# Both gate pieces side by side in products of 64 columns, also for the fourth quarter of the chunks

## The chip, the cores and the metric

The kernel runs on one core of one Trainium2 chip. The metric is the device time of one execution in microseconds (us), lower being better. Five engines of the core run their own instruction streams and meet at semaphores: TensorE (PE in the rows, its weight loads PEld) multiplies matrices, VectorE (DVE) and ScalarE (ACT) work elementwise, GpSimd (POOL) helps a little, SyncE (SP) starts the DMAs.

## The reference

The program is a chain of three transformer blocks on 256 tokens of width 1024 in float32. The change lies in the mixture of experts that the second block applies twice (two layers). Each layer has 16,384 experts, numbered by a pair of keys out of 128 x 128. For each token, 8 heads choose 16 experts each:

```python
def peer_ffn(h, wq, keys, u, v):            # shortened
    q = (h @ wq).reshape(B, S, PEER_HEADS, 2, half)
    s1, s2 = scores of both halves of q against the two sets of 128 keys
    v1, i1 = lax.top_k(s1, PEER_TOPK); v2, i2 = lax.top_k(s2, PEER_TOPK)
    sc, j = lax.top_k(every v1 + v2, PEER_TOPK)
    experts = e1 * PEER_NKEYS + e2          # the two key numbers that j picks
    gates = jax.nn.softmax(sc, axis=-1)
    act = gelu(einsum('td,ted->te', h, u[experts]))
    return einsum('te,ted->td', gates * act, v[experts])
```

## The kernel before, in words

The kernel does not gather experts. It computes `gelu(h @ u)` for all 16,384 of them in 128 chunks of 128 experts (the experts lie on the partitions, the 256 tokens in the free dimension), multiplies each value by the gate of its expert and token, which is zero for nearly all, and multiplies the result with `v`. The class `Experts` is that stage; there are two in the program.

**Halves.** The stage has 256 steps, called halves: 128 "in" halves that make hidden chunks from `u`, and 128 "out" halves that add a hidden chunk times `v` to the sums in `acc`. `expert_order` puts in 0 to 63 first, then out c and in c + 64 in turn, then out 64 to 127. Every float32 weight is split in a high and a low part (`w_hi` by ScalarE, L1116; `w_lo` by VectorE, L1124), and each product is made of three. The split weights lie in a ring of three buffers: ScalarE's highs of half g wait until TensorE has begun what follows half g - 3 (`halves_used`). The hidden chunk of an out half is split too: its high by ScalarE (L2157), its low by VectorE (L2190), one half ahead.

**Gates.** The gates must become a dense array of experts x tokens. The chunks are taken in four quarters of 32 chunks, and the tokens in 16 batches of 16. For a batch VectorE builds one-hots in fp16 (`build`, L2244 to L2255): `hot2`, 128 columns per token, says which second key each of the token's 128 chosen pairs has, and `hot1`, 32 columns per token, holds the gate at the pair's first key. The gate is split in two fp16 pieces, so there are two arrays `hot1`. TensorE multiplies them token by token (`spread`, L2121): the result, for a token 128 experts x 32 chunks, is the sum over both pieces. Three halves later VectorE multiplies it into the hidden values (`multiply`, L2258).

**Two forms.** In quarters 0 and 3 (counting from 0) a token takes two products of 32 columns that add up in PSUM, 32 products for a batch in one bank, batches alternating between banks 2 and 3. VectorE multiplies straight from PSUM. In the quarters of `BESIDE`, 1 and 2, a token takes one product of 64 columns, both pieces side by side, 16 products for a batch, 8 tokens in each of banks 2 and 3. ScalarE copies the second pieces to SBUF (`take_seconds`, L2206), VectorE adds the first pieces from PSUM to them into `whole` (L2266, once per bank), and the product with the hidden values reads `whole` (L2276).

**When.** `__init__` (L2012) lays the 16 batches of a quarter evenly between the last in half that the quarter needs and the first out half that uses it. Quarter 3 has halves 195 to 219 for that, 24 halves, all of them out halves; quarters 1 and 2 have 56. A batch is built by VectorE in its step g, spread by TensorE after half g, and multiplied in VectorE's step g + 3. The spread waits for the one-hots and for its bank: the semaphore `gated` counts what VectorE has read out of the banks (`lay_out_banks`, L2038, works out the counts). In each step VectorE does in turn: lows of the half (L1124), hidden low of the next (L2190), the sum of a returned in chunk (L2195, only up to half 193), multiply, build.

Of the kernel before, what the change touches and what calls it, by code (L numbers as in the profile page):

```python
# [73 lines left out]
class Chip:  # L74


    def __init__(self, ctx, nc):
# [64 lines left out]
        self.onehots_made = ctx.enter_context(nc.semaphore("onehots_made"))  # L142
        self.gate_banks = ctx.enter_context(nc.semaphore("gate_banks_filled"))
        self.seconds_out = ctx.enter_context(nc.semaphore("second_pieces_out"))
        self.quarters_gated = ctx.enter_context(nc.semaphore("quarters_gated"))
        self.gated = ctx.enter_context(nc.semaphore("hidden_gated"))
        self.heads_normed = ctx.enter_context(nc.semaphore("heads_normed"))
        self.heads_gated_early = ctx.enter_context(nc.semaphore("heads_gated_by_pool"))
# [94 lines left out]
class Stage:  # L243
# [19 lines left out]
    def scalar(self, act):  # L263
        pass
# [815 lines left out]
class SplitWeights(Stage):  # L1080
# [6 lines left out]
    QUARTER = HALF_SLOT // 2  # L1087
# [884 lines left out]
QUARTER = CHUNKS // 4  # L1972
BATCH = BANK // QUARTER
BATCHES = S // BATCH
# [12 lines left out]
class Experts(SplitWeights):  # L1987
# [2 lines left out]
    WIDEN_AT = 15  # L1990
    EXP_AT = 23
    TURN_AFTER = 33
    BESIDE = (1, 2)

    def __init__(self, k, route, found, hidden, gate, rest, places, pairs, pieces, hot1, hot2, mask, whole,
                 second):
# [41 lines left out]
    def lay_out_banks(self):  # L2038
# [3 lines left out]
        for q in range(4):  # L2042
            for b in range(BATCHES):
                n = 2 if q in self.BESIDE else 1
                for half in range(n):
# [75 lines left out]
    def spread(self, pe, q, b):  # L2121
        k = self.k
        pe.wait_ge(k.onehots_made, self.batches_through(q, b))
        for first, n, bank, free, units, through in self.fills[q, b]:
            if free:
                pe.wait_ge(k.gated, free)
            for j in range(first, first + n):
                hot2, hot1 = self.hot2[b % 2][:, j, :], self.hot1[b % 2]
                if q in self.BESIDE:
                    w = PIECES * QUARTER  # L2130
# [14 lines left out]
    def scalar(self, act):  # L2145
        k = self.k
        for g in range(self.n + 2):
            if self.ahead <= g < self.n:
                self.split_high(act, g)
            if g + 1 < self.n and self.halves[g + 1][0] == "out":  # L2150
                c = self.halves[g + 1][1]
                if c % QUARTER == 0:
                    if c // QUARTER in self.BESIDE:
                        act.wait_ge(k.quarters_gated, self.number * len(self.BESIDE) + 1 + self.BESIDE.index(c // QUARTER))
                    else:
                        act.wait_ge(k.gated, self.units_through[c // QUARTER, BATCHES - 1])
                act.activation(self.top(c), self.place(c), ACT.Copy).then_inc(k.tops_made, 1)  # L2157
            for q, batch in self.spread_after[g - 3]:
                if q in self.BESIDE:
                    self.take_seconds(act, q, batch)  # L2160
            if self.WIDEN_AT <= g < self.WIDEN_AT + 8:
                self.route.widen(act, g - self.WIDEN_AT)
            if g == self.EXP_AT:
                self.route.scalar(act)
            if 2 <= g and self.halves[g - 2][0] == "in":
                c = self.halves[g - 2][1]
                act.wait_ge(k.hidden_banks, self.chunks_before() + c + 1)
                if c < PLACES:
                    act.activation(self.place(c), k.bank[:, c % 2, 0:S], ACT.Gelu).then_inc(k.hidden_made, 1)  # L2169
                else:  # L2170
                    act.activation(self.place(c), k.bank[:, c % 2, S:2 * S], ACT.Copy).then_inc(k.hidden_rests, 1)  # L2171
            if 3 <= g and self.halves[g - 3][0] == "in" and self.halves[g - 3][1] >= PLACES:
                c = self.halves[g - 3][1]
                act.wait_ge(k.hidden_added, self.added_through(c))
                act.activation(self.place(c), self.place(c), ACT.Gelu).then_inc(k.hidden_made, 1)

    def vector(self, dve):
# [3 lines left out]
        for g in range(self.n):  # L2181
# [18 lines left out]
                self.build(dve, q, batch)  # L2200
            self.sum_step(dve, g)

    def seconds_through(self, q, b):
        return 2 * (BATCHES * (self.number * len(self.BESIDE) + self.BESIDE.index(q)) + b + 1)

    def take_seconds(self, act, q, b):  # L2206
        k = self.k
# [50 lines left out]
    def multiply(self, dve, q, b):  # L2258
        k = self.k
        first = q * QUARTER % PLACES  # L2260
        for t, n, bank, free, units, through in self.fills[q, b]:
            dve.wait_ge(k.gate_banks, through)
            if q in self.BESIDE:
                pieces = k.bank[:, bank, :].rearrange("p (t i n) -> p i t n", t=n, i=PIECES)
                dve.wait_ge(k.seconds_out, self.seconds_through(q, b) + (t > 0) - 1)
                dve.tensor_tensor(self.whole[:, t:t + n, :], pieces[:, 0], self.second[:, t:t + n, :],  # L2266
                                  ALU.add).then_inc(k.gated, units)
        if b == 0:
            dve.wait_ge(k.hidden_made, self.chunks_before() + (q + 1) * QUARTER)
        hidden = self.hidden[:, first:first + QUARTER, b * BATCH:(b + 1) * BATCH]  # L2270
        if q in self.BESIDE:
            dve.wait_ge(k.gated, self.units_through[q, b])
            gates = self.whole.rearrange("p t n -> p n t")
        else:
            gates = k.bank[:, 2 + b % 2, :].rearrange("p (t i) -> p i t", t=BATCH)
        ins = dve.scalar_tensor_tensor(hidden, gates, 1.0 / GATE_SCALE, hidden, ALU.mult, ALU.mult)  # L2276
        if q not in self.BESIDE:
            ins.then_inc(k.gated, 2)
        elif b == BATCHES - 1:
            ins.then_inc(k.quarters_gated, 1)  # L2280

# [1551 lines left out]
```

## Time and profile before

| what | value |
|---|---|
| median of 3 timed runs | 3816.76 us (3811.96 to 3827.05) |
| the profiled execution's own time | 3812.13 us |
| its span, first to last instruction | 3810.3 us |
| mean granted TensorE clock | 0.968 |
| ScalarE, busy share of the span | 54% |
| out halves and gates of quarter 3, first stage | 2104 to 2192 us |
| the same in the second stage | 3094 to 3182 us |

A share of busy time is an average over many stages with different limits. For a change in one place one reads the windows and the order of time there. Times in rows are microseconds from the start of the span; an instruction's duration holds its start-up and drain, so that the distance between the starts of two neighbours is what one of them costs its engine.

### The profile page before, as it was taken

Reading aid. Unit: us, or ns where it says so; the run is one execution under the profiler, and the core shown is the slowest. Engines: PE = TensorE matmul, PEld = TensorE weight load, DVE = VectorE, ACT = ScalarE, POOL = GpSimd, SP = SyncE. Lnnn points to the kernel's source line nnn. Section 1 sums busy time; section 2 is a strip of 40 time slices with the busy share of each in tenths; the row PEclk is TensorE's granted clock in tenths of the full one; section 3 lists DMA queues with packets and bytes.
Section 4 is the critical chain, followed back from the end, with each engine's and each line's share of the span. In section 5 each row is a group of like instructions: output and inputs, shape, how many; then the busy total and the mean of one; then the engine's idle time right before and its main releaser. Section 6 shows DMA issues by size and latency. Waiting matters only on the chain. (4 is left out here: it accounts for less than half of the span.)

```text
span 3810.3 us, 59916 instructions
## 1 busy us (share of the span) xinstructions
PE 3637.0 (95%) x22328; PEld 3116.2 (82%) x22328; DVE 3061.5 (80%) x6382; ACT 2060.6 (54%) x4449; POOL 122.1 (3%) x112
## 2 busy tenths in 40 slices
PE   6999999999889979999999999999999999999898
PEld 5887788887778767998888887799988888888687
DVE  7887688887678776988888956689798997788766
ACT  3554555555355545545656456554555655555455
POOL 0000000000000000400000000050000000000000
PEclk9999999999789989999999999999999999999899
DMA  8767375766247523544454454254455545686354
GB/s 325 277 243 287 125 295 209 299 221 240 100 181 268 213 85 138 184 156 177 178 185 180 166 188 156 78 177 159 174 177 179 181 172 178 232 308 261 122 188 155
DMA packets 119619, 744.52 MB, mean 195 GB/s; under 512 B 13857, under 2 KB 14273, under 8 KB 44833
## 3 DMA queue, kind: packets, MB, share of 16 engines
q1 hardware_dynamic: 118082, 737.57, 52.9%
q8 instruction: 178, 2.92, 0.3%
q10 hardware_dynamic: 416, 2.06, 0.1%
q0 software_dynamic: 832, 1.06, 0.1%
q14 instruction: 111, 0.91, 0.1%
HBM read 738.53 MB, written 1.05 MB: 194 GB/s over the span
## 5 line engine op out<-in xcount | busy, mean ns | idle before, releaser
L212 PE MATMUL bank<-h_split,weights_high 128*128 128x512 f32 (+1 forms) x5824 | 1714.7, 358 | 15.5 <-DVE h_split L723 9.4
L1116 ACT ACTIVATE weights_high<-weight_ring 128x512 fp32r<-128x512 f32 x2248 | 1292.6, 624 | 650.9 <-PE bank L212 377.1
L1124 DVE TENSOR_TENSOR weights_low<-weight_ring,weights_high 128x512 fp32r<-128x512 f32 x2168 | 1394.9, 687 | 274.5 <-ACT weights_high L1116 252.9
L212 PE MATMUL bank<-h_split,weights_low 128*128 128x256 f32 x4800 | 1269.2, 280 | 0.0
L212 PEld LDWEIGHTS bank<-h_split,weights_high 128*128 128x128 f32 x5824 | 1014.8, 189 | 163.4 <-issue 16.7
L212 PEld LDWEIGHTS bank<-h_split,weights_low 128*128 128x128 f32 x4800 | 911.1, 190 | 37.8
L212 PE MATMUL acc<-weights_high,hidden_high 128*128 128x512 f32 x1552 | 613.8, 395 | 2.6 <-DVE hidden_low L1298 2.4
L212 PE MATMUL acc<-weights_high,hidden_low 128*128 128x512 f32 x1552 | 605.0, 390 | 0.0
L212 PE MATMUL acc<-weights_low,hidden_high 128*128 128x512 f32 x1552 | 604.5, 390 | 0.0
L212 PEld LDWEIGHTS acc<-weights_high,hidden_low 128*128 128x128 f32 x1552 | 291.3, 188 | 63.9
L212 PEld LDWEIGHTS acc<-weights_low,hidden_high 128*128 128x128 f32 x1552 | 291.7, 188 | 59.8 <-issue 0.2
L212 PEld LDWEIGHTS acc<-weights_high,hidden_high 128*128 128x128 f32 x1552 | 291.3, 188 | 56.2 <-issue 4.2
L1263 ACT ACTIVATE work<-bank 128x256 f32<-128x256 f32 x264 | 101.8, 386 | 344.9 <-PE bank L212 344.9
L212 PE MATMUL bank<-weights_high,h_split 128*128 128x512 f32 x704 | 222.8, 395 | 7.4 <-DVEq L234 2.9
L212 PEld LDWEIGHTS bank<-weights_high,h_split 128*128 128x128 f32 x704 | 133.6, 190 | 38.8 <-DVEq L234 3.9
L2249 DVE TENSOR_TENSOR h_tok<-h_feat,work 128x2048 f16<-128x2048 f16 x128 | 156.0, 1219 | 0.0
L2169 ACT ACTIVATE work<-bank 128x256 f32<-128x256 f32 x128 | 49.2, 384 | 193.2 <-PE bank L212 193.2
L212 PE MATMUL bank<-work 128*128 128x64 f32 (+10 forms) x896 | 125.6, 333 | 19.5 <-ACTq L234 8.3
L212 PE MATMUL bank<-weights_low,h_split 128*128 128x512 f32 x352 | 138.3, 393 | 0.0
L212 PEld LDWEIGHTS bank<-work 128*128 128x128 f32 (+5 forms) x896 | 108.0, 213 | 35.4 <-ACTq L234 11.1
L2171 ACT ACTIVATE work<-bank 128x256 f32<-128x256 f32 x128 | 49.3, 385 | 141.2 <-PE bank L212 141.2
L348 DVE SCALAR_TENSOR_TENSOR mod_sums<-h_tok,columns,mod_sums 128x512 f32<-128x512 f32 x160 | 112.5, 746 | 15.5 <-DMA h_tok<-slots 14.8
(347 smaller groups left out, 3522.1 us busy)
## 6 DMA issues: line engine op xcount, KB each, us to landing
weight_ring<-stream SPq DMA_DIRECT2D x574, 1024.0 KB, 4.8
h_feat<-slots SPq DMA_DIRECT2D x96, 512.0 KB, 5.8
h_tok<-slots SPq DMA_DIRECT2D x94, 512.0 KB, 5.9
work<-slots SPq DMA_DIRECT2D x26, 512.0 KB, 8.4
mod_sums<-biases SPq DMA_DIRECT2D x7, 1536.0 KB
h_feat<-rows SPq DMA_DIRECT2D x8, 512.0 KB, 3.8
work<-rows SPq DMA_DIRECT2D x7, 512.0 KB, 4.7
work<-biases SPq DMA_DIRECT2D x1, 1536.0 KB
```

Source lines behind the costliest of these rows:

```text
L212: ins = self.nc.tensor.matmul(out, lhs, rhs, start=start, stop=stop)
L348: ins = dve.scalar_tensor_tensor(self.sums.where[:, a], k.buffers[self.buffer][:, h * BANK:(h + 1) * BANK], c, self.sums.where[:, a], ALU. ...
L1116: act.activation(k.w_hi[:, b, q * self.QUARTER:(q + 1) * self.QUARTER], self.raw(g, q), ACT.Copy).then_inc(k.highs_ready, 1)
L1124: return eng.tensor_tensor(k.w_lo[:, b, w], self.raw(g, q), k.w_hi[:, b, w].bitcast(F32), ALU.subtract)
L1263: act.activation(self.rests[:, part, :], self.bank_of(c, part)[:, S:2 * S], ACT.Copy).then_inc(k.scalar_for_vector.sem, k.scalar_for_vecto ...
L2169: act.activation(self.place(c), k.bank[:, c % 2, 0:S], ACT.Gelu).then_inc(k.hidden_made, 1)
L2171: act.activation(self.place(c), k.bank[:, c % 2, S:2 * S], ACT.Copy).then_inc(k.hidden_rests, 1)
L2249: dve.tensor_tensor(cut(hot2), grid(self.places, N_KEYS), spread(self.pairs[:, S + b * BATCH:S + (b + 1) * BATCH, :], N_KEYS), ALU.is_equal)
```

## The change

`BESIDE` becomes (1, 2, 3): quarter 3 takes the form of quarters 1 and 2. Per stage, for 16 batches, that is 256 products of 64 columns in place of 512 of 32, 32 copies by ScalarE that were not there, 32 sums by VectorE that were not there, and 16 products by VectorE that read `whole` in SBUF where they read PSUM. Every batch of the quarter fills both banks.

The semaphore `quarters_gated` (one signal per quarter) is replaced by `sums_gated` (one per batch). Before the first sum of a batch VectorE now waits until its product of the batch before has read `whole`, and ScalarE waits on the same semaphore before the first out chunk of a quarter.

```diff
-        self.quarters_gated = ctx.enter_context(nc.semaphore("quarters_gated"))
+        self.sums_gated = ctx.enter_context(nc.semaphore("summed_gates_used"))
...
-    BESIDE = (1, 2)
+    BESIDE = (1, 2, 3)
...
-                        act.wait_ge(k.quarters_gated, self.number * len(self.BESIDE) + 1 + self.BESIDE.index(c // QUARTER))
+                        act.wait_ge(k.sums_gated, self.sums_through(c // QUARTER, BATCHES - 1))
...
+    def sums_through(self, q, b):
+        return BATCHES * (self.number * len(self.BESIDE) + self.BESIDE.index(q)) + b + 1
...
+                if t == 0 and self.sums_through(q, b) > 1:
+                    dve.wait_ge(k.sums_gated, self.sums_through(q, b) - 1)
...
-        elif b == BATCHES - 1:
-            ins.then_inc(k.quarters_gated, 1)
+        else:
+            ins.then_inc(k.sums_gated, 1)
```

VectorE in the fourth quarter, one step with a multiply and a build. First before; `work<-bank,work` is the product with the hidden values, `h_tok` is `hot2`:

```order
L1124 TENSOR_TENSOR weights_low<-weight_ring,weights_high 128x512 [waits highs_ready] x2
L2190 TENSOR_TENSOR hidden_low<-work,hidden_high 128x256 [waits weighted_highs_made]
L2276 SCALAR_TENSOR_TENSOR work<-bank,work 128x32x16 [waits gate_banks_filled]
L2244 TENSOR_TENSOR work<-h_feat,work 128x512
L2249 TENSOR_TENSOR h_tok<-h_feat,work 128x2048 [waits gate_banks_filled]
L2255 TENSOR_TENSOR work<-work 128x16x32 [waits dve_step]
L2255 TENSOR_TENSOR work<-work 128x16x32
```

The same step in the changed kernel, where line numbers are up to 5 higher:

```order
L1124 TENSOR_TENSOR weights_low<-weight_ring,weights_high 128x512 [waits highs_ready] x2
L2190 TENSOR_TENSOR hidden_low<-work,hidden_high 128x256 [waits weighted_highs_made]
L2271 TENSOR_TENSOR work<-bank,work 128x256 [waits second_pieces_out,summed_gates_used,gate_banks_filled]
L2271 TENSOR_TENSOR work<-bank,work 128x256 [waits second_pieces_out,gate_banks_filled]
L2281 SCALAR_TENSOR_TENSOR work<-work 128x32x16 [waits hidden_gated]
L2247 TENSOR_TENSOR work<-h_feat,work 128x512
L2252 TENSOR_TENSOR h_tok<-h_feat,work 128x2048 [waits gate_banks_filled]
L2258 TENSOR_TENSOR work<-work 128x16x32 [waits dve_step]
L2258 TENSOR_TENSOR work<-work 128x16x32
```

Two sums have come ahead of the product, which reads SBUF alone, and three waits with them. The steps around stand as they stood.

TensorE in the fourth quarter between two out halves, before; `work,h_tok` are the one-hots:

```order
L212 MATMUL acc<-weights_high,hidden_low 128x512
L212 MATMUL bank<-work,h_tok 128x32 [waits hidden_gated,onehots_made]
L212 MATMUL bank<-work,h_tok 128x32 x31
L212 MATMUL acc<-weights_high,hidden_high 128x512 [waits weighted_lows_made,first_lows_by_vector]
L212 MATMUL acc<-weights_low,hidden_high 128x512
```

And in the changed kernel:

```order
L212 MATMUL acc<-weights_high,hidden_low 128x512
L212 MATMUL bank<-work,h_tok 128x64 [waits hidden_gated,onehots_made]
L212 MATMUL bank<-work,h_tok 128x64 x7
L212 MATMUL bank<-work,h_tok 128x64 [waits hidden_gated]
L212 MATMUL bank<-work,h_tok 128x64 x7
L212 MATMUL acc<-weights_high,hidden_high 128x512 [waits weighted_lows_made,first_lows_by_vector]
```

The 32 products are 16, in two groups of which each waits for its bank. The name of the wait is the same, but its count is another: it was that of the batch two before, and is that of the batch just before.

## Rows read from the trace of the kernel before

**Rows 1.** The page: busy time, share of the span, instructions.

```profile
PE 3637.0 (95%) x22328; PEld 3116.2 (82%) x22328; DVE 3061.5 (80%) x6382; ACT 2060.6 (54%) x4449; POOL 122.1 (3%) x112
```

**Rows 2.** Windows: stretch, us, busy (count) of each engine, clock, DMA share, GB/s.

```profile
2113.30:2180.10 66.80, 66.80 (x659) 54.72 (x658) 66.52 (x126) 29.21 (x60) 0.00 (x0) 1.00 0.44 159
2104.39:2189.93 85.54, 85.54 (x826) 70.05 (x824) 83.69 (x158) 38.58 (x80) 0.00 (x0) 1.00 0.46 165
3093.92:3179.47 85.55, 85.55 (x826) 70.05 (x825) 83.69 (x158) 38.59 (x80) 0.00 (x0) 1.00 0.44 165
```

**Rows 3.** Order of time on TensorE, fourth quarter: start, duration, what, count.

```profile
2129.65 0.39 PE L212 MATMUL acc<-weights_high,hidden_low 128*128 128x512 f32 x1
2129.88 0.96 PE L212 MATMUL bank<-work,h_tok 128*128 128x32 f16 x32
2130.69 0.47 PE L212 MATMUL acc<-weights_high,hidden_high 128*128 128x512 f32 x1
2131.01 0.39 PE L212 MATMUL acc<-weights_low,hidden_high 128*128 128x512 f32 x1
```

**Rows 4.** Order of time on VectorE, fourth quarter, idle time before in brackets.

```profile
2111.75 1.29 DVE L1124 TENSOR_TENSOR weights_low<-weight_ring,weights_high 128x512 fp32r<-128x512 f32 x2
...
2113.29 0.69 DVE L2276 SCALAR_TENSOR_TENSOR work<-bank,work 128x512 f32<-128x512 f32 x1
2113.89 0.41 DVE L2244 TENSOR_TENSOR work<-h_feat,work 128x512 f16<-128x512 f16 x1
...
2116.03 1.29 DVE L1124 TENSOR_TENSOR weights_low<-weight_ring,weights_high 128x512 fp32r<-128x512 f32 x2
...
2181.09 1.29 DVE L1124 TENSOR_TENSOR weights_low<-weight_ring,weights_high 128x512 fp32r<-128x512 f32 x2 [0.28 <-ACT weights_high L1116]
2186.32 0.69 DVE L2276 SCALAR_TENSOR_TENSOR work<-bank,work 128x512 f32<-128x512 f32 x1
...
2189.98 1.29 DVE L1124 TENSOR_TENSOR weights_low<-weight_ring,weights_high 128x512 fp32r<-128x512 f32 x2 [0.89 <-ACT weights_high L1116]
```

**Rows 5.** Order of time on VectorE in the third quarter.

```profile
2023.67 0.42 DVE L2195 TENSOR_TENSOR work<-bank,work 128x256 f32<-128x256 f32 x1 [1.35 <-ACT work L2171]
2024.01 0.74 DVE L2266 TENSOR_TENSOR work<-bank,work 128x256 f32<-128x256 f32 x2
2024.79 1.11 DVE L2276 SCALAR_TENSOR_TENSOR work<-work 128x512 f32<-128x512 f32 x1
2025.81 1.29 DVE L1124 TENSOR_TENSOR weights_low<-weight_ring,weights_high 128x512 fp32r<-128x512 f32 x2
```

**Rows 6.** Order of time on TensorE in the second quarter.

```profile
1735.46 0.64 PE L212 MATMUL bank<-work,h_tok 128*128 128x64 f16 x16
1735.94 0.48 PE L212 MATMUL acc<-weights_high,hidden_high 128*128 128x512 f32 x1
```

**Rows 7.** Line 2212: minimum, median, maximum in ns, first and last start.

```profile
L2212 ACT ACTIVATE work<-bank x128: 360/375/387, 1737.0 to 3078.6; 128x256 f32<-128x256 f32 x128
```

**Rows 8.** Order of time on ScalarE, fourth quarter.

```profile
2130.17 1.15 ACT L1116 ACTIVATE weights_high<-weight_ring 128x512 fp32r<-128x512 f32 x2 [1.06 <-PE bank L212]
```

**Rows 9.** TensorE behind the spread of batch 1: half 2 begins.

```profile
2114.31 0.47 PE L212 MATMUL acc<-weights_high,hidden_high 128*128 128x512 f32 x1
```

**Rows 10.** TensorE behind the last spread: half 25 begins.

```profile
2189.85 0.47 PE L212 MATMUL acc<-weights_high,hidden_high 128*128 128x512 f32 x1
```

**Rows 11.** VectorE behind the quarter; one row of a repeated pattern.

```profile
2199.27 1.29 DVE L1124 TENSOR_TENSOR weights_low<-weight_ring,weights_high 128x512 fp32r<-128x512 f32 x2 [1.09 <-ACT weights_high L1116]
```

**Rows 12.** Windows with and behind an idle piece of TensorE.

```profile
2294.40:2296.80 2.40, 0.57 (x3) 0.52 (x4) 2.00 (x4) 2.37 (x6) 0.00 (x0) 0.99 0.00 0
2296.80:2300.20 3.40, 3.40 (x10) 2.63 (x9) 2.89 (x5) 0.64 (x2) 0.00 (x0) 0.50 0.54 164
```

**Rows 13.** Line 2276: minimum, median, maximum in ns, first and last start.

```profile
L2276 DVE SCALAR_TENSOR_TENSOR work<-bank,work x64: 676/684/689, 1639.5 to 3181.1; 128x512 f32<-128x512 f32 x64
L2276 DVE SCALAR_TENSOR_TENSOR work<-work x64: 1103/1114/1140, 1738.7 to 3079.9; 128x512 f32<-128x512 f32 x64
```

More of the change, by code:

```diff
@@ L2201, in vector @@
             self.sum_step(dve, g)
+    def sums_through(self, q, b):
+        return BATCHES * (self.number * len(self.BESIDE) + self.BESIDE.index(q)) + b + 1
     def seconds_through(self, q, b):
-        return 2 * (BATCHES * (self.number * len(self.BESIDE) + self.BESIDE.index(q)) + b + 1)
+        return 2 * self.sums_through(q, b)
     def take_seconds(self, act, q, b):
```

## The prediction

> **What bounds the kernel now.** I read the page's busy times first, then the windows, then the order of time on each engine.
>
> The page has TensorE busy for 95% of the span and VectorE for 80% [rows 1]. That says which engine is short on average, and not which one is short where the change acts. The change acts on the fourth quarter of the chunks in both expert stages. The windows there show both engines full: in 66.80 us TensorE is busy for all of it and VectorE for 66.52, while ScalarE has 29.21 [rows 2]. The second expert stage reads the same: the window of 85.54 us and its twin of 85.55 us hold the same 826 matmuls and 158 VectorE instructions, with 83.69 us of VectorE each [rows 2]. So I work out one stage and double it.
>
> In order of time TensorE runs without a gap through that stretch: 12 products of a half, and after 16 of 24 halves the 32 small products of a batch [rows 3]. VectorE also has almost no gap, and its rows repeat per half: two weight lows and a hidden low, then, where a batch falls due, the multiply (L2276) and the building of one-hots (L2244 to L2255) [rows 4]. TensorE sets the pace, by a hair. The reader is to see that VectorE has no room at this place: its idle pieces in the stretch are like the one of 0.28 us, and reach 0.89 only at the end [rows 4].
>
> **Why this quarter is tight.** I count halves of the stretch from 0, the one after which the first of the 16 batches is spread (half 195 of the stage). The code spaces batches by 24/15 halves, so they are spread after halves 0, 1, 3, 4, 6, 8, 9, 11, 12, 14, 16, 17, 19, 20, 22, 24, and multiplied in VectorE's step three halves on (3, 4, 6, ... 27). In quarters two and three, which already have the new form, the spacing is 56/15 halves, and VectorE has idle pieces of 1.35 us there [rows 5].
>
> **The costs, each from a distance between starts.**
>
> - VectorE, lows and hidden low of a half: 2111.75 to 2113.29 is 1.54 us. Build of a batch: 2113.89 to 2116.03 is 2.14. Multiply of the old form: 2113.29 to 2113.89 is 0.60 [rows 4].
> - Multiply of the new form, in the third quarter: 2024.01 (two sums) to 2025.81 (the next work) is 1.80: 0.78 for two sums and the wait on them, 1.02 for the product that reads both operands from SBUF [rows 5]. VectorE therefore gains 1.20 us of work per batch, 19.2 per stage.
> - TensorE, half: 2114.31 to 2189.85 holds 23 halves and 14 batches [rows 9, 10], (75.54 - 14 x 0.90) / 23 = 2.74. The 0.90 is the small products of a batch, old form: 2129.88 to 2130.69 is 0.81, and the next product is 0.09 late (2130.69 to 2131.01 is 0.32, where 0.23 is usual), so 0.90 [rows 3]. New form: 2×8 products, 1735.46 to 1735.94 is 0.48, with the same 0.09, so 0.57 [rows 6]. It saves 0.33 per batch.
> - ScalarE: two copies more per batch, 0.375 us each [rows 7], on an engine with 37 us idle in 66.8 [rows 2]. They stand behind the weight highs and the hidden high of the same step. In the fourth quarter ScalarE has 1.06 or more idle after those [rows 8]. I cost them at nothing; if that cover went, one copy (0.375) per batch would be late, 6 us per stage.
> - The wait on the last product before a new sum: the product is at least one half's lows (1.54) old by then. In the third quarter the two satisfied waits before the first sum leave it 0.34 behind its predecessor (2023.67 to 2024.01) [rows 5], as without a wait. Nothing, there and here.
> - The ring of small-product banks: a batch of the new form fills both banks, so it waits for the sums of the batch just before; a batch of the old form alternates and waits for the one two before. Behind the waiting TensorE instruction stand all later halves, and ScalarE's next weight highs wait for those. This wait is what carries VectorE's load to TensorE. Batch 1 is spread after half 1, but the sums of batch 0 come in VectorE's step 3.
>
> **The sum.** Start where both kernels agree. In the old form half 2 begins at 2114.31, behind the small products of batch 1 [rows 9]. In the new form these wait for the second sum of batch 0, which ends 0.74 after 2113.29, and eight products take 0.24: half 2 begins at 2114.3. No loss yet, and no gain from the shorter products.
>
> From there the last spread that waits is batch 15 (after half 24), on the sums of batch 14 in VectorE's step 25. Between the multiplies of batches 0 and 14 VectorE does 14 multiplies x 1.80 = 25.2, 14 builds x 2.14 = 30.0 and 22 halves' lows x 1.54 = 33.9: 89.0 us. TensorE today needs 2114.31 to 2189.85 = 75.5 for the same halves [rows 9, 10]. So half 25 begins 13.5 us later. The same count with 0.60 in place of 1.80 gives 72.2, against 73.03 between the starts 2113.29 and 2186.32 [rows 4]; the method is 0.8 us off by the idle pieces.
>
> Then TensorE has its pace back: halves 25 and 26 take 2.74 each, and VectorE's two remaining steps with one multiply (1.54 + 1.54 + 1.80) fit beside them. Nothing returns the time later, since halves 29 and on are paced by TensorE, with VectorE idle 1.09 in each [rows 11]. VectorE could also be made to wait for weight highs, which need TensorE to begin what follows the half three before. At batch 3 (after half 4) its products wait for the sums of batch 2 in VectorE's step 6, at 2113.29 + 1.80 + 2.14 + 1.54 (step 4) + 1.80 + 2.14 + 1.54 (step 5) + 1.54 = 2125.8, done at 2126.2. ScalarE starts 0.29 after such products do (2129.88 to 2130.17) and has two pieces in 1.15 [rows 3, 8], the first at 2127.1; VectorE wants it at its step 7, 1.80 + 2.14 later than 2125.8, at 2129.7. The margin is 2.6 us, and at batch 6, the other long wait, it is the same. Two stages: 27 us.
>
> **What TensorE's waits cost besides.** TensorE would idle 89.0 - 23 x 2.74 - 14 x 0.57 = 18.0 us per stage, mostly in five gaps of about 3 to 3.6 us (before batches 3, 6, 8, 11, 13, which are the ones due two steps behind). The trace shows what such a gap does: TensorE has 0.57 us of work in 2.40 us, and then a granted clock of 0.50 for 3.40 us [rows 12]. That is the 1.2 GHz level, and loses 1.7 us of TensorE's work; for a longer gap I allow twice that, 3.4. From below it costs nothing, since the next wait is as long as the loss; from above, all ten gaps at 3.4 us add up to 34. I take 2 us for both stages, near the lower end, since a loss shortens the gap behind it. The page "TensorE: Matmul & The Clock Gate" of the Trainium skill (Part 1) has the same behaviour as its rule, an idle array being throttled to half rate; it speaks against this change, and the trace agrees with its direction.
>
> The sum: 3812.13 (profiled execution, 1.8 over its span) + 27 + 2 = 3841. The three timed runs of before have a median of 3816.76, 4.6 above it; I predict 3842.
>
> **One price where the Trainium skill differs.** The trace has the product from PSUM at a median of 684 ns and the same product from SBUF alone at 1114 ns, 64 of each [rows 13]. "VectorE: DVE Perf Modes" (the section on the TRN2 errata) gives fp32 from PSUM the larger fixed cost, 120 cycles against 58. By it the move to SBUF would be free; the row decides. The sum without that extra is the third rival.
>
> **The rivals.**
>
> 1. Faster. TensorE sets the pace and its products shrink by 0.33 us in each of 32 batches: 3812.1 - 10.6 = 3801.5. For it: TensorE has no idle time in the stretch, and VectorE stands at 80% overall. Against it: 66.52 of 66.80. It decides if VectorE's 1.20 us per batch fit beside; they need 19.2 us, and 85.5 - 83.7 = 1.9 are free [rows 2].
> 2. Much slower: the gaps before the products lower TensorE's clock, and the losses add up instead of vanishing in the next wait: 3841 + 32 = 3873 at the most, 3857 if half do.
> 3. Less slow: the product from SBUF costs 0.60 here, since it reads differently than in the third quarter. Then the multiply is 1.38, the sum 89.0 - 14 x 0.42 = 83.2, the loss 7.6 per stage: 3827. Against it: all 64 rows lie within 1103 and 1140.
> 4. The change does not reach the path: the waits for banks are met because TensorE lags. Then nothing changes, 3812 to 3817. Against it: VectorE's step 25 would have to be early, with 16.8 us more work ahead of it.
>
> **How the numbers follow.** Forecast 0.79; rival 1 0.04, rival 2 0.08, rival 3 0.05, rival 4 0.04. A measurement tells this kernel from no change by about 0.5%, 19 us: below 3798 and above 3836. The forecast's own range is 3834 to 3852 (24 to 34 us for the two stages' sum, and the 4.6 between execution and median); some 0.05 of it falls under 3836. Slower: 0.74 + 0.08 + a little of rival 3 = 0.83. Faster: 0.04. Same: 0.13. The range for 8 in 10 takes in rival 3 and half of rival 2: 3825 to 3858.
>
> **What would show it.** In the profile after: the fourth quarter is 13 to 15 us longer in each stage (about 99 where 85.5 stood), with VectorE busy over 98% and TensorE near 80%; TensorE waits before small products on the sums, five times over 2 us per stage; the product from SBUF is there 32 times more at 1.11 us; the clock reads 0.50 for some microseconds inside; all other stages are unchanged. Wrong if VectorE shows idle pieces on weight highs in that quarter (then the ring of waits is tighter than its load), if TensorE shows no waits there, or if the clock stays low past the quarter.

## The result and the profile after

| | before | changed |
|---|---|---|
| median of 7 timed runs | 3812.28 us (3807.51 to 3827.83) | 3844.57 us (3838.93 to 3859.42) |
| ratio, 95% interval | | 1.0083 (1.0056 to 1.0109) |
| the profiled execution | 3812.13 us | 3844.57 us |
| S of the first and second expert stage | 75.53, 75.53 us | 89.93, 89.08 us |

The change makes the kernel 0.83% slower, some 32 us. S is the measure of all that follows: the time on TensorE from the start of half 2 to the start of half 25 of the fourth quarter, as the prediction counts them. It is read to 0.01 us in one profile, while whole executions of one kernel scatter by 20 us. The like stretch of the first quarter, which is the same in every kernel of this document, measures 72.80 us in each of them.

The page of the changed kernel, against [rows 1]. TensorE has 512 matmuls fewer, VectorE 64 instructions more and 36 us more to do, and the shares hardly moved:

```profile
PE 3638.8 (95%) x21816; PEld 3113.4 (81%) x21816; DVE 3097.8 (81%) x6446; ACT 2082.2 (54%) x4513; POOL 122.0 (3%) x112
```

The windows over S in both stages of the changed kernel (columns as in [rows 2]):

```profile
2122.34:2212.27 89.93, 74.66 (x507) 59.51 (x503) 89.45 (x166) 41.24 (x98) 0.00 (x0) 0.96 0.39 134
3124.68:3213.77 89.09, 76.36 (x507) 60.64 (x503) 88.61 (x165) 41.26 (x98) 0.00 (x0) 0.94 0.38 137
```

VectorE is busy for all but 0.48 us of each. TensorE, which had no idle time there in [rows 2], works for 74.7 of 89.9 and 76.4 of 89.1 us. Who waits for whom in the first of the two windows (total us, times, the longest; VectorE has no row, so it waits for nobody):

```profile
ACT weights_high L1116 <- PE bank L212: 34.6, 15, 5.0
PEld bank L212 <- issue: 19.9, 14, 3.9
ACT weights_high L1116 <- PE acc L212: 16.1, 9, 2.8
PE bank L212 <- DVE work L2271: 15.3, 7, 3.5
```

The last row is where the loss shows: TensorE waits 15.3 us for VectorE's sums. Add 3.4 us that it loses at half clock (below) and take off the 14 x 0.33 = 4.6 that its products have become shorter, and 14.1 of the 14.4 us by which this S is longer are accounted for. In order of time, the small products of batch 3 of the first stage, where the old form has no gap (compare [rows 3]):

```profile
2130.97 0.39 PE L212 MATMUL acc<-weights_high,hidden_low 128*128 128x512 f32 x1
2134.42 0.65 PE L212 MATMUL bank<-work,h_tok 128*128 128x64 f16 x16 [3.06 <-DVE work L2271]
2134.90 0.47 PE L212 MATMUL acc<-weights_high,hidden_high 128*128 128x512 f32 x1
```

VectorE in the same stretch, against [rows 4]: no row has an idle piece. The multiply in these rows is 2126.86 to 2128.64, that is 1.78 where 0.60 stood; a build 2.13; lows and hidden low 1.54. The last row is the pair of sums that batch 3 waits for; it begins as soon as VectorE gets to it, and the products begin at 2134.42, behind the first sum:

```profile
2125.32 1.28 DVE L1124 TENSOR_TENSOR weights_low<-weight_ring,weights_high 128x512 fp32r<-128x512 f32 x2
2126.52 0.41 DVE L2190 TENSOR_TENSOR hidden_low<-work,hidden_high 128x256 fp32r<-128x256 f32 x1
2126.86 0.74 DVE L2271 TENSOR_TENSOR work<-bank,work 128x256 f32<-128x256 f32 x2
2127.63 1.09 DVE L2281 SCALAR_TENSOR_TENSOR work<-work 128x512 f32<-128x512 f32 x1
2128.64 0.41 DVE L2247 TENSOR_TENSOR work<-h_feat,work 128x512 f16<-128x512 f16 x1
2128.97 1.22 DVE L2252 TENSOR_TENSOR h_tok<-h_feat,work 128x2048 f16<-128x2048 f16 x1
2130.10 0.75 DVE L2258 TENSOR_TENSOR work<-work 128x512 f16<-128x512 f16 x2
2130.77 1.29 DVE L1124 TENSOR_TENSOR weights_low<-weight_ring,weights_high 128x512 fp32r<-128x512 f32 x2
...
2132.31 1.29 DVE L1124 TENSOR_TENSOR weights_low<-weight_ring,weights_high 128x512 fp32r<-128x512 f32 x2
2133.52 0.42 DVE L2190 TENSOR_TENSOR hidden_low<-work,hidden_high 128x256 fp32r<-128x256 f32 x1
2133.85 0.75 DVE L2271 TENSOR_TENSOR work<-bank,work 128x256 f32<-128x256 f32 x2
```

ScalarE's copies lie where the prediction put them, behind the highs, with idle time before the next ones (compare [rows 8]):

```profile
2140.74 1.16 ACT L1116 ACTIVATE weights_high<-weight_ring 128x512 fp32r<-128x512 f32 x2 [1.07 <-PE bank L212]
2141.80 0.40 ACT L2157 ACTIVATE hidden_high<-work 128x256 fp32r<-128x256 f32 x1
2142.11 0.64 ACT L2215 ACTIVATE work<-bank 128x256 f32<-128x256 f32 x2
2144.25 1.16 ACT L1116 ACTIVATE weights_high<-weight_ring 128x512 fp32r<-128x512 f32 x2 [1.50 <-PE acc L212]
```

And the clock. Windows of the changed kernel around two waits of TensorE (3.55 us before batch 6, 2.98 before batch 13):

```profile
2150.40:2153.40 3.00, 0.00 (x0) 0.00 (x0) 3.00 (x7) 0.00 (x0) 0.00 (x0) 1.00 0.01 3
2153.40:2156.80 3.40, 2.89 (x21) 2.54 (x22) 3.37 (x7) 2.00 (x5) 0.00 (x0) 0.50 0.33 43
2195.40:2197.80 2.40, 0.03 (x1) 0.00 (x0) 2.40 (x6) 0.00 (x0) 0.00 (x0) 1.00 0.66 277
2197.80:2201.20 3.40, 2.79 (x21) 2.43 (x22) 3.37 (x7) 2.00 (x5) 0.00 (x0) 0.50 0.02 5
```

TensorE idles through the first and third window, and in the second and fourth it runs at 0.50, the 1.2 GHz level. That makes 6.8 us at half rate in S of the first stage and 10.2 us in the second.

**Where the 32 us are.** The same instruction on TensorE, before and after, gives the shift from the front of the span. It is 8.0 us at the first small products of the fourth quarter of the first stage (2109.85 and 2117.85), and 7.9 already at 1491 us, ahead of any expert stage, where no instruction differs: these two executions differ there by that much on their own. From there to half 25 it grows by 14.4 us (2189.85 and 2212.27). In the second stage it goes from 20.8 (3099.39 and 3120.19) to 34.4 (3179.38 and 3213.77), by 13.6. Nothing of it comes back behind the quarter: the shift is 22.42 at half 25 of the first stage and still 22.44 a hundred microseconds later. The two quarters account for 28.0 of the 32.5 us between the spans; the rest arises in stretches where no instruction differs, and is scatter.

### The profile page after: what moved, and what is told of

Same layout as the page of the kernel before. It is cut to its first block and busy times, and to the rows that moved or that the text cites. A ratio compares the mean times of both kernels' runs of the same rounds, so it can differ in the third digit from the quotient of the medians.

```text
span 3842.8 us, 59118 instructions
## 1 busy us (share of the span) xinstructions
PE 3638.8 (95%) x21816; PEld 3113.4 (81%) x21816; DVE 3097.8 (81%) x6446; ACT 2082.2 (54%) x4513; POOL 122.0 (3%) x112
## 5 line engine op out<-in xcount | busy, mean ns | idle before, releaser
L2171 ACT ACTIVATE work<-bank 128x256 f32<-128x256 f32 x128 | 49.4, 386 | 140.8 <-PE bank L212 140.8
```

## The experiments

Each has one execution with a profile. The whole times hold the scatter named above, so the verdicts are on S.

### The new semaphore alone

```diff
-    BESIDE = (1, 2, 3)
+    BESIDE = (1, 2)
```

(on the changed kernel)

> The new semaphore alone: the fourth quarter keeps the old form, and the second and third quarters have the new wait of VectorE on the product of the batch before. All theories measure S, the time on TensorE from the start of half 2 to the start of half 25 of the fourth quarter: 75.5 us before, 89.9 and 89.1 us in the changed kernel. Theory (VectorE's added load of 1.2 us per batch sets the pace): S is 75.5 in both stages, and the third quarter is as before. Rival (the wait itself costs, in every quarter that has it): S is 75.5 too, but the stretch of the second and third quarter is over 1 us longer per stage and VectorE shows idle time on its own semaphore.

S is 75.53 in both stages, the same to the last digit as before:

```profile
2117.33:2192.86 75.53, 75.53 (x731) 61.86 (x727) 73.76 (x138) 33.59 (x70) 0.00 (x0) 1.00 0.46 161
3106.87:3182.40 75.53, 75.53 (x730) 61.85 (x727) 73.77 (x138) 33.59 (x70) 0.00 (x0) 1.00 0.45 162
```

The like stretch of the second and third quarter (the half behind batch 1 to the half behind batch 15) is 155.62 and 155.58 us, with 155.60 and 155.59 before. VectorE's list of waits between 1740 and 2110 us has ScalarE's copies of the in chunks (L2171) and its weight highs in it, and not its own semaphore. The wait costs nothing.

### The tighter ring of banks alone

```diff
                     freed[bank] = units
+                    if q == 3 and n == 1:
+                        freed[5 - bank] = units
```

(on the kernel before)

> The kernel before, but in the fourth quarter every batch of small products also waits for the multiply of the batch just before, as it would if it filled both banks: the tighter ring without the load. Theory (load): the multiplies of batches due two steps behind come 0.2 to 0.7 us after TensorE is ready for the next small products, so S grows from 75.5 by 2 to 4 us. Rival (the ring by itself costs the time, VectorE's load is a bystander): S is near 89.

S is 76.33 and 76.38: 0.8 us more, less than either side expected, and the profile shows a single wait of TensorE of 0.5 us. The ring alone is not the cost. The changed kernel's list of waits would have misled here: all of TensorE's waits stand there in the row of the ring's semaphore.

### Product of the fourth quarter cut to an eighth

```diff
+        if q == 3:
+            hidden, gates = hidden[:, :, 0:2], gates[:, :, 0:2]
         ins = dve.scalar_tensor_tensor(hidden, gates, 1.0 / GATE_SCALE, hidden, ALU.mult, ALU.mult)
```

> The changed kernel, but in the fourth quarter VectorE's product covers 2 of a batch's 16 tokens (so the hidden values of the others are not gated in that quarter): the full ring, the sums and ScalarE's copies stay, the product falls from 1.02 us to about 0.15. Theory (load): the multiply is 0.93, S = 14 x 0.93 + 30.0 + 33.9 = 76.9, within 1 us. Rival (ring): near 89, since all waits stay. Rival (ScalarE's copies are late): S stays over 82.

S is 78.22 in both stages: 11 us of the loss are gone with one operation of VectorE, all waits being as in the changed kernel. The 1.3 above the 76.9 worked out are these, VectorE's waits between 2110 and 2200:

```profile
DVE weights_low L1124 <- ACT weights_high L1116: 1.3, 2, 1.0
```

At this load the two engines are nearly level (TensorE would need 71.0), and then each waits for the other now and then.

### The sums done twice

```diff
+                if q == 3:
+                    spare = (self.rest if t else self.gate).rearrange("p (t n) -> p t n", n=QUARTER)
+                    dve.tensor_tensor(spare, pieces[:, 0], self.second[:, t:t + n, :], ALU.add)
                 dve.tensor_tensor(self.whole[:, t:t + n, :], pieces[:, 0], self.second[:, t:t + n, :],
```

> The changed kernel with each of VectorE's sums of the fourth quarter done a second time into a spare tile: 0.68 us more of VectorE's work per batch, nothing else. Theory (load): S grows by 14 x 0.68 = 9.5 over the changed kernel, to about 98.8. Rival (TensorE's clock or the ring sets the pace, VectorE has room left): S grows by less than 3. The granted clock tells a third: if its drops add up, it falls below 1.00 for longer and S passes 101.

```profile
2114.30:2212.79 98.49, 80.67 (x507) 63.17 (x503) 98.01 (x193) 41.21 (x98) 0.00 (x0) 0.91 0.36 129
3127.66:3226.94 99.28, 82.56 (x506) 64.91 (x503) 98.80 (x194) 40.84 (x98) 0.00 (x0) 0.88 0.35 121
```

98.5 and 99.3 against 98.8. Every microsecond given to VectorE is paid in full (9.4 and 10.2 more for the 9.5 added). The clock falls further, to a mean of 0.91 and 0.88 over the stretch (17 and 24 us at half rate), and still the time is the one of VectorE's load within 0.5 us: TensorE's slack takes the slower halves up.

### The load alone, in the old form

```diff
+        if q == 3:
+            flat = k.bank[:, 2 + b % 2, :].rearrange("p (t n) -> p t n", n=QUARTER)
+            if b:
+                dve.wait_ge(k.dve_step, self.spared)
+            for t in (0, BATCH // 2):
+                at = slice(t, t + BATCH // 2)
+                dve.tensor_tensor(self.whole[:, at, :], flat[:, at], self.second[:, at, :], ALU.add)
+            spare = self.rest.rearrange("p (t n) -> p t n", n=QUARTER)
+            dve.tensor_tensor(spare, flat[:, 0:BATCH // 2], self.second[:, 0:BATCH // 2, :], ALU.add).then_inc(k.dve_step, 1)
+            self.spared = k.step("dve")
         ins = dve.scalar_tensor_tensor(hidden, gates, 1.0 / GATE_SCALE, hidden, ALU.mult, ALU.mult)
```

(on the kernel before: 32-column products, alternating banks, no copies by ScalarE)

> The kernel before (old form and old ring in the fourth quarter), with three more sums of 128x256 by VectorE per batch of that quarter, ahead of the multiply and into tiles that nobody reads there: 3 x 0.34 = 1.02 us more per batch, so a multiply of 1.62. Theory (the load alone does it, with or without the new ring, the 64-column products and ScalarE's copies): VectorE has 14 x 1.62 + 30.0 + 33.9 = 86.6 us to do and S is 86.6, within 1.5. Rival (the load needs the tighter ring to reach TensorE, or ScalarE's copies): S stays under 80.

```profile
2129.97:2214.90 84.93, 81.17 (x731) 64.35 (x727) 84.93 (x176) 33.60 (x70) 0.00 (x0) 0.96 0.41 144
```

S is 84.93 in both stages, VectorE busy without a break. It is 1.7 below the 86.6 expected, just past the margin, and the end of the stretch says why:

```profile
2209.87 1.30 DVE L1124 TENSOR_TENSOR weights_low<-weight_ring,weights_high 128x512 fp32r<-128x512 f32 x2
```
```profile
2211.22 0.50 PE L212 MATMUL acc<-weights_high,hidden_high 128*128 128x512 f32 x1
2214.08 0.96 PE L212 MATMUL bank<-work,h_tok 128*128 128x32 f16 x32
```

With alternating banks batch 15 (2214.08) does not wait, neither for a bank nor for its one-hots. TensorE is held up for the last time at half 24 (2211.22), by VectorE's lows of that half, and runs on for 3.7 us to half 25. VectorE's work in the path is then 14 multiplies of 1.60, 13 builds, 20 halves' lows and the two lows of half 24, 82.3 us from the first multiply, which begins 1.0 before half 2: 82.3 - 1.0 + 3.7 = 85.0. The load makes 9.4 us of loss by itself; form, ring and copies are not needed for it. What carries it to TensorE is another thing here: the listed waits are 2.1 us for one-hots and 1.4 for weight lows, and none for a bank.

### Turned tile of summed gates

```diff
-    whole, second = room(BATCH, QUARTER), room(BATCH, QUARTER)
+    whole, second = room(QUARTER, BATCH).rearrange("p n t -> p t n"), room(BATCH, QUARTER)
```

> The changed kernel with the tile of summed gates laid out chunk by token, so that VectorE's product reads it in one run per row instead of 512 values 128 bytes apart; the sums write it spread out instead. S is 89.0 to 89.9 in the changed kernel. If the 1.02 us of the product from SBUF comes from the spread-out reads, it falls to near the 0.60 of the product from PSUM and S to 89.0 - 14 x 0.42 = 83.2. If it comes from two operands in SBUF alone, as in the other products of this kernel, it stays and S stays 89. If the spread-out writes cost the sums as much, S stays 89 too and the sums' rows show it.

Line 2281 and line 2271 of this run (minimum, median, maximum in ns):

```profile
L2281 DVE SCALAR_TENSOR_TENSOR work<-work x96: 691/693/695, 1755.6 to 3222.6; 128x512 f32<-128x512 f32 x96
L2281 DVE SCALAR_TENSOR_TENSOR work<-bank,work x32: 684/685/693, 1656.1 to 2730.7; 128x512 f32<-128x512 f32 x32
```
```profile
L2271 DVE TENSOR_TENSOR work<-bank,work x192: 579/605/637, 1754.5 to 3222.0; 128x256 f32<-128x256 f32 x192
```

Both answers at once. The product falls from 1115 to 693 ns, about what it costs from PSUM (685). But PSUM is read with the same stride: in both forms the gates of a chunk lie 32 values, 128 bytes, apart. So the extra is neither the memory nor the stride by itself, but this stride in SBUF. And the sums rise from 416 to 605 ns with their spread-out writes. By distances between starts, averaged over the 15 multiplies of the window, a sum goes from 0.39 to 0.54 and the product from 1.02 to 0.61, so the multiply from 1.81 to 1.69: 14 x 0.12 = 1.7. S is 87.44 and 87.48, 1.6 less than the changed kernel's 89.1. "SBUF — State Buffer" of the Trainium skill ("Door 1: The DMA port swizzle") has it as a rule that consecutive accesses within a 16-byte line of SBUF run at full rate and each step to a new line pays. The trace agrees for VectorE's reads (1115 against 693 ns) and for its writes (605 against 416).

### One sum in place of two

```diff
+        if q == 3:
+            dve.wait_ge(k.gate_banks, self.units_through[q, b])
+            dve.wait_ge(k.sums_gated, self.sums_through(q, b) - 1)
+            dve.wait_ge(k.seconds_out, self.seconds_through(q, b))
+            both = k.bank[:, 2:4, :].rearrange("p a n -> p (a n)").rearrange("p (t i n) -> p i t n", i=PIECES, n=QUARTER)
+            dve.tensor_tensor(self.whole, both[:, 0], self.second, ALU.add).then_inc(k.gated, 2)
...
```

> The changed kernel with one sum of 128x512 over both banks in place of two of 128x256 in the fourth quarter. If a VectorE instruction costs its elements at 0.26 us per 256 and the rest is a fixed part, the two sums with their 0.78 become about 0.60 and S = 89.0 - 14 x 0.18 = 86.5. Rival (the earlier release of the first bank by the first of two sums is worth more): S is 89 or over, since TensorE's first 8 products wait for the whole sum.

```profile
2141.66 0.69 DVE L2269 TENSOR_TENSOR work<-bank,work 128x512 f32<-128x512 f32 x1
2142.38 1.05 DVE L2287 SCALAR_TENSOR_TENSOR work<-work 128x512 f32<-128x512 f32 x1
```

S is 88.14 in both stages: a gain of 1.0, not 2.6. The sum with the wait on it takes 0.72 (2141.66 to 2142.38) where two took 0.78; I had put the whole of the 0.18 down to a second start. A sum that nothing waits on costs 0.33 in the run above with the load alone. In the changed kernel the first sum of a pair costs 0.33 too and the second, which the product waits on, 0.45; so 0.12 of the 0.78 is that wait, and it stays.

### Weight lows given to GpSimd

Two edits, the second with both pieces of a low (`BY_POOL = (0, 1)`), and one with the turned tile besides:

```diff
+    LATE, BY_POOL = range(196, 223), (1,)
...
+        for g in self.LATE:
+            for q in self.BY_POOL:
+                ins = self.low_piece(pool, g, q)
+            ins.then_inc(k.lows_by_pool, 1)
...
+            if g in self.LATE:
+                pe.wait_ge(k.lows_by_pool, self.pool_base + self.POOL_HALVES + g - self.LATE[0] + 1)
```

(and VectorE makes the pieces that are left)

> The changed kernel with GpSimd making the second of the two weight lows of a half in halves 196 to 222 (a piece takes 1.30 us there, 0.60 on VectorE), so 0.60 us less of VectorE's work per half. Theory (load): S = 89.0 - 22 x 0.60 = 75.8, near the kernel before. Rival (ring): S stays near 89. A third: the two engines slow each other while both work on SBUF, then VectorE's fp16 builds are over 2.14 us and S lies between.

> The same with GpSimd making both weight lows of those halves: VectorE's work falls by 1.20 per half to 25.2 + 30.0 + 22 x 0.34 = 62.7 us, less than the 71.0 that TensorE needs for 23 halves of 2.74 and 14 batches of 0.57. Theory: TensorE sets the pace, S is 71 to 73, less than the 75.5 of the kernel before. Rivals: GpSimd, at 2.6 us per half plus its start behind ScalarE's highs, becomes the bound (then S is over 76 and TensorE waits for its lows), or slows VectorE (builds over 2.14 us).

> The turned tile of summed gates and GpSimd's second weight low together. By the loads: 89.0 - 22 x 0.60 - 14 x 0.42 = 69.9 for VectorE if both edits do all they can, so TensorE's 71.0 is the bound and S is 71 to 73; if the turned tile brings nothing, S is as with GpSimd's help alone, near 75.8. Rival (ring): near 89.

S is 99.1, 108.9 (110.6 in the second stage) and 96.1: all slower than the changed kernel, where by the load all three were to win the time back. The whole executions, 3874, 3884 and 3868 us, are above those of the changed kernel as well. The windows over S with one and with both pieces on GpSimd:

```profile
2133.53:2232.64 99.11, 80.64 (x505) 63.77 (x502) 98.63 (x143) 41.10 (x98) 45.45 (x23) 0.90 0.36 128
```
```profile
2118.37:2227.27 108.90, 82.44 (x505) 65.00 (x502) 108.41 (x121) 40.83 (x98) 68.38 (x46) 0.90 0.32 110
```

VectorE has 23 and 45 instructions fewer and is busy for longer. Its order of time and GpSimd's, with one piece:

```profile
2140.23 1.47 DVE L2263 TENSOR_TENSOR work<-h_feat,work 128x512 f16<-128x512 f16 x1
2141.63 1.22 DVE L2268 TENSOR_TENSOR h_tok<-h_feat,work 128x2048 f16<-128x2048 f16 x1
2142.77 1.85 DVE L2274 TENSOR_TENSOR work<-work 128x512 f16<-128x512 f16 x2
...
2154.16 1.73 DVE L1124 TENSOR_TENSOR weights_low<-weight_ring,weights_high 128x512 fp32r<-128x512 f32 x1
```
```profile
2139.61 1.82 POOL L1124 TENSOR_TENSOR weights_low<-weight_ring,weights_high 128x512 fp32r<-128x512 f32 x1 [3.80 <-ACT weights_high L1116]
2142.16 1.83 POOL L1124 TENSOR_TENSOR weights_low<-weight_ring,weights_high 128x512 fp32r<-128x512 f32 x1 [0.74 <-ACT weights_high L1116]
```

GpSimd's first piece runs to 2141.43. VectorE's instruction of 0.41 us that begins at 2140.23 ends at 2141.70, just behind it. The next, of 1.22, begins in GpSimd's pause and takes 1.22, though the second piece begins under it at 2142.16; that piece takes 1.83 where 1.30 is usual, so it ends 1.30 behind 2142.69, about where VectorE's ends. Those of VectorE from 2142.77 then meet the second piece. So in these rows the one that starts first runs at its own time and the other ends late. The low of 0.68 us at 2154.16 takes 1.73. VectorE stands about 1.1 us in each of these, and GpSimd's pieces take 1.29 to 4.98 us, 1.98 on the average over the window. The third possibility of the first expectation came true, and stronger than it said. VectorE's time is 99.1 where its load is 75.8, so each of 23 pieces costs it 1.0 us; with both pieces it is 108.9 where the load is 62.7, again 1.0 for each of 46. A piece takes 0.60 off VectorE: the help costs more than the work it takes. TensorE waits on VectorE's sums and not on GpSimd in all three (18.4 us in the first). The "GPSIMD Engine Reference" of the Trainium skill (1. Specifications) says that GpSimd shares its SBUF interfaces with VectorE and meets its instructions with two SBUF inputs; the trace agrees, and it puts the price at 1.0 us of a piece that takes 1.30 alone.

### The changed kernel once more

> The changed kernel once more. In its first profile S was 89.93 in the first expert stage and 89.08 in the second, where VectorE's load is 89.04. If the 0.9 is the granted clock (two drops to 0.50 in each of the windows, at other places), S is again 89.0 to 90.5 and any excess over 89.1 stands where a drop fell into halves that no wait follows. If the first stage has a load of its own that the second has not, the same stage is again 0.9 longer.

S is 89.14 and 89.09, with 10.2 us at half rate in each. The 0.9 of the first profile's first stage was the clock: its second drop (the fourth window above) slows the halves behind batch 13, and in that execution the two batches left (14 and 15) came without a wait behind slower halves. From the products of batch 13 to those of batch 15 it is 13.38 us (2198.41 to 2211.79), and 12.48 in the second stage (3200.80 to 3213.28), where they run at full clock: these are the 0.9. The row of batch 15:

```profile
2211.56 0.39 PE L212 MATMUL acc<-weights_high,hidden_low 128*128 128x512 f32 x1
2211.79 0.64 PE L212 MATMUL bank<-work,h_tok 128*128 128x64 f16 x16
```

In the repeat the drops come after the gaps before batches 3, 6 and 11, and each is followed by a wait that takes it up.

## Why the prediction was right

- **Which engine is short.** Predicted: VectorE, over 98% busy in the quarter, TensorE near 80%. Measured: 99.5%, and 83 to 86%. Three experiments move S as VectorE's load says: the sums done twice add 9.4 and 10.2 us where 9.5 were worked out, the small product gives 78.22 where the load is 76.9 and VectorE waits 1.3, and the load alone in the old form gives 84.93 where 85.0 come out.
- **The sum.** Predicted: 89.0 us for the stretch, 13.5 more. Measured: 89.93 and 89.08, repeated 89.14 and 89.09. The multiply was taken from the third quarter at 1.80 and is 1.81 on the average over the window.
- **Where both kernels agree.** Half 2 begins 4.46 us behind the start of batch 0's products before (2109.85 to 2114.31) and 4.49 after (2117.85 to 2122.34): no loss yet and none of the saved 0.33, as said.
- **The waits.** Predicted: 18.0 us per stage, five of them over 2 us. Measured: 15.3 us in 7 waits in the first stage, four of them over 2 us, and 12.7 us in 7 waits in the second, three over 2 us. In place of the rest stand the slower halves: 6.8 and 10.2 us at half clock are 3.4 and 5.1 us of work. The gap before batch 8 shows it: 1.64 and 1.39 us where about 3 were forecast, behind a drop at batch 6.
- **The clock.** 2 us were added for it over both stages, near the lower end of 0 to 34. Measured: 0.9 in one stage of four seen, nothing in the others, while the clock was at half rate for 6.8 to 10.2 us in each. The reason given, that a loss shortens the gap behind it, is what the waits show.
- **The price of the product from SBUF.** The size was right, and what makes it was not known. The prediction read the row (1114 against 684) as SBUF against PSUM, set it against the comparison of the two in "VectorE: DVE Perf Modes" of the Trainium skill (the section on the TRN2 errata), and let the row decide. The turned tile shows that the 1114 belongs to reads 128 bytes apart in SBUF: in one run the product costs 693 from SBUF, and PSUM with the same stride costs 685. The number held here because the fourth quarter has the layout of the rows it came from.
- **The whole.** 3842 was predicted and 3844.57 measured. The two quarters were predicted at 27 us and 2 for the clock, and measured at 28.0; the rest of the agreement is luck within a scatter of 20 us.

## What to carry to other kernels

Look for the engine that is short in the stretch that changes, not in the span: an edit that saves 0.33 us per batch on the engine that is busy 95% overall cost 1.2 us on the one that was busy 99.6% just there. Work per turn times turns, between two points where both kernels agree, then gave the loss to within 1 us, and the same count says beforehand that a form for which VectorE has the time in a roomy quarter (56 halves for 16 batches) does not fit in a tight one (24). Whether it pays in the roomy ones no run here shows. In a list of waits the row names the semaphore that was late and not the reason: relax or tighten the wait and change the load apart from each other before naming either. None of the versions tried has a shorter S than the kernel before; of these, the fourth quarter is best left in the old form.

## What the runs showed of the hardware

- VectorE and GpSimd, both at work on SBUF: VectorE's instructions with two SBUF inputs, of 2 or of 4 bytes, that came second ended only behind GpSimd's (0.41 to 1.47, 0.68 to 1.73 us), and GpSimd's piece of 1.30, where it came second, ended late in turn (1.83 in the rows above). VectorE's sums with one operand in PSUM took 0.41 to 0.44 in the ten cases that overlap a piece in the first two of these runs.
- A VectorE product of 128x512 takes 693 ns with its second operand in one run in SBUF, 1115 with it 128 bytes apart in SBUF, and 684 with it 128 bytes apart in PSUM; a sum of 128x256 takes 416 with a contiguous and 605 with a spread-out target in SBUF.
- A VectorE instruction that waits on the one just before it begins 0.12 us later than one that does not (0.45 against 0.33 behind a sum of 128x256).
- TensorE's granted clock fell to 0.50 for 3.4 us behind waits of 2.4 to 3.6 us, but not behind each: in the first profile it stayed at 1.00 behind waits of 3.06 and 3.52 us (batches 3 and 11 of the first stage), and fell behind one of 2.54 (batch 6 of the second). Half rate for up to 24 of 99 us cost at most 0.5 us where TensorE would have waited anyway.
